# Linear attention: the value mask moved behind a page pair, the sum over sequences moved between two chunk states, the first half of the scores scaled behind the head loop in two parts

## What is computed

```python
k, v = mla_keys_values(cache_ckv_l[phys], cache_kpe_l[phys], kpos, w_ukv, g_kh)
sc = jnp.einsum('bthd,bkhd->bhtk', q, k).astype(jnp.float32) * scale
m_new = jnp.maximum(m, sc.max(axis=-1))
p = jnp.exp(sc - m_new[..., None])
```

```python
inter = jnp.einsum('bthk,bhkv->bthv', qc * jnp.exp(b), s)
s = jnp.exp(bl)[..., None] * s + jnp.einsum('bshk,bshv->bhkv', kc * jnp.exp(bl[:, None] - b), vc)
```

## Time and profile before

| | before |
|---|---|
| median of 3 runs | 1000.68 us (1000.61 to 1001.48) |
| profiled execution, its own time | 1000.3 us |
| its span, first to last instruction | 998.3 us |
| TensorE (PE) busy | 957.6 us, 96% |
| VectorE (DVE) busy | 632.2 us, 63% |
| ScalarE (ACT) busy | 473.9 us, 47% |
| GpSimd (POOL) busy | 129.0 us, 13% |
| TensorE's share of the chain that ended last | 73% |
| VectorE's, GpSimd's share of it | 10%, 5% |

### The profile page before, as it was taken

How to read it: one execution, slowest core, us unless ns; L and a number is a source line. 1 busy time by engine, 2 the same in 40 slices (tenths; PEclk the granted TensorE clock), 3 DMA queues, 4 the chain that set the end, 5 groups by cost and what they waited for, 6 DMA issues and landing times.

```text
span 998.3 us, 17683 instructions
## 1 busy us (share of the span) xinstructions
PE 957.6 (96%) x6795; PEld 880.8 (88%) x6795; DVE 632.2 (63%) x1140; ACT 473.9 (47%) x834; POOL 129.0 (13%) x220
## 2 busy tenths in 40 slices
PE   6999999989998999999999898899999999999997
PEld 6998478787886799999999776799999999999997
DVE  5653897787875479855664743756756766444454
ACT  6433566653442457643434473124755555333353
POOL 3420140000132300000003079100000000000000
PEclk9999999999989999999999999556999999999999
DMA  8570032321258634444444205000343444344431
GB/s 321 202 300 27 17 102 73 112 70 43 96 166 279 232 133 165 167 169 169 169 169 161 93 2 211 11 1 1 138 160 149 170 169 170 137 160 157 158 151 48
DMA packets 34485, 135.42 MB, mean 136 GB/s; under 512 B 5273, under 2 KB 17433, under 8 KB 21858
## 3 DMA queue, kind: packets, MB, share of 16 engines
q1 hardware_dynamic: 28370, 117.37, 32.4%
q0 software_dynamic: 6032, 16.92, 5.1%
HBM read 130.11 MB, written 4.17 MB: 135 GB/s over the span
## 4 chain that ended last, share of the span: by engine, by line
PE 73%; DVE 10%; POOL 5%; issue 5%; ACT 3%; DMA 2%; POOLq 1%; SPq 0%; DVEq 0%; ACTq 0%
PE ps L902 18%; PE ps L904 18%; PE ps L903 18%; POOL arena L805 4%; PE ps L1450 3%; DMA ring<-in_stream 2%; PE ps L1107 1%; PE ps L1458 1%; PE ps L1108 1%; PE ps L1467 1%; PE ps L1109 1%; PE ps L1466 1%; POOLq L726 1%; PE ps L1030 1%; DVE arena L2182 1%
## 5 line engine op out<-in xcount | busy, mean ns | idle before, releaser
L904 PE MATMUL ps<-a2hi_split,ring_split 128*128 128x288 f32 x512 | 150.5, 294 | 0.0
L904 PEld LDWEIGHTS ps<-a2hi_split,ring_split 128*128 128x128 f32 x512 | 96.4, 188 | 0.0
L902 PE MATMUL ps<-nhi_split,hi_split 128*128 128x288 f32 x320 | 95.1, 297 | 0.1
L904 PE MATMUL ps<-nhi_split,ring_split 128*128 128x288 f32 x320 | 94.1, 294 | 0.0
L1992 DVE TENSOR_TENSOR ring_split<-ring,hi_split 128x2048 fp32r<-128x2048 f32 x36 | 82.2, 2286 | 17.8 <-ACT hi_split L1562 17.8
L1562 ACT ACTIVATE hi_split<-ring 128x2048 fp32r<-128x2048 f32 x36 | 68.7, 1910 | 31.9 <-PE ps L904 22.7
L1107 PE MATMUL ps<-sq_split,hT_split 128*128 128x288 f32 (+1 forms) x256 | 78.5, 307 | 5.3 <-DVE pages_lo_split L2164 3.3
L902 PE MATMUL ps<-up_nhi_split,up_hi_split 128*128 128x288 f32 x256 | 76.2, 298 | 0.5 <-DVE arena L2388 0.5
L902 PE MATMUL ps<-a2hi_split,hi_split 128*128 128x288 f32 x256 | 75.8, 296 | 0.0
L1108 PE MATMUL ps<-wuk_lo_split,hT_split 128*128 128x288 f32 (+1 forms) x256 | 75.6, 295 | 0.0
L1562 ACT ACTIVATE up_hi_split<-ring 128x2048 fp32r<-128x2048 f32 x28 | 53.6, 1913 | 46.4 <-PE ps L904 44.7
(11 more groups left out here) (430 smaller groups left out, 2629.8 us busy)
## 6 DMA issues: line engine op xcount, KB each, us to landing
ring<-in_stream SPq DMA_DIRECT2D x96, 1024.0 KB, 4.9
arena<-in_ckvT SPq DMA_DIRECT2D x64, 128.0 KB, 2.1
arena<-in_ckv POOLq DMA_DIRECT2D x26, 128.0 KB, 3.0
ring<-in_ckv POOLq DMA_DIRECT2D x21, 128.0 KB, 2.4
arena<-in_wu POOLq DMA_DIRECT2D x1, 2240.0 KB, 10.0
arena<-in_ckv SPq DMA_DIRECT2D x17, 128.0 KB, 2.9
arena<-in_s POOLq DMA_DIRECT2D x4, 512.0 KB, 4.2
out_gla_s<-arena POOLq DMA_DIRECT2D x4, 512.0 KB, 3.4
```

What stands on the lines that cost most here:

```text
L902: pe.matmul(ps[:, 0:T], wh[:, k, col:col + P], xh, start=first and k == which[0], stop=False)
L904: mm = pe.matmul(ps[:, 0:T], wl[:, k, col:col + P], xh, start=False, stop=last and k == which[-1])
```

## The change

Only VectorE's program changes. Three steps move, none is added or taken away, and no data moves elsewhere:

```diff
-            V.tensor_tensor(vmask, bc(gv[:, 2, 0:GD].unsqueeze(1), [P, NS, GD]), bc(cst("seqmask").unsqueeze(2), [P, NS, GD]), ALU.mult).then_inc(vmask_ready, 1)
             for c in range(2):
...
                                 ALU.mult).then_inc(bank_of(("cross", c)), 1)
-            for c in range(2):
-                copied(dve, ("cross", c))
-            V.tensor_reduce(crossed, own.rearrange("p b v -> p v b"), AX.X, ALU.add).then_inc(crossed_ready, 1)
             for h in range(GH):
 
                 if h == 2:
+                    for c in range(2):
+                        copied(dve, ("cross", c))
+                    V.tensor_reduce(crossed, own.rearrange("p b v -> p v b"), AX.X, ALU.add).then_inc(crossed_ready, 1)
                     key_sums(18, 19)
...
             key_sums(19, 20)
+            V.tensor_tensor(vmask, bc(gv[:, 2, 0:GD].unsqueeze(1), [P, NS, GD]), bc(cst("seqmask").unsqueeze(2), [P, NS, GD]), ALU.mult).then_inc(vmask_ready, 1)
...
-            def scaled_scores(c):
+            def scaled_scores(c, between=(0, 0)):
...
                 link(w)
+                key_sums(*between)
                 m = mx[:, P * c:P * c + P]
...
-                if h == 2:
-                    scaled_scores(0)
...
-            key_sums(24, 29)
+            key_sums(24, 25)
+            scaled_scores(0, (25, 26))
+            key_sums(26, 29)
             maxima(0)
```

## The result

The changed kernel took 974.32 us (971.87 to 975.37) against 1001.08 (1000.61 to 1004.0) beside it, a ratio of 0.9723 with a 95% interval of 0.9697 to 0.975. I had forecast 995.5, and 993.2 as the lower end: the sign was right, the size was not, and nearly all of the gain lies where I had not looked. One fact is needed to read this number, and I only learned it from later comparisons: **both kernels have two outcomes**, one execution after the other on the same chip. Of 101 executions of the kernel before, 58 took 1000.4 to 1007.1 us and 43 took 973.3 to 980.3; of 28 of the changed one, 4 took 999.2 to 1001.1, one 987.4, and 23 took 971.4 to 975.4. The comparison above sets the upper outcome of one against the lower outcome of the other. Between like outcomes the ratio was 0.9964 (0.9942 to 0.9985) in one later comparison and 0.9969 (0.9949 to 0.9989) in another: some 3 us.

What follows compares the result with a forecast made beforehand. It took VectorE's early scores, ahead of GpSimd's page queue and TensorE's pairs, as the bound. Both paths gain about 5.5 us, 4.9 after the weights; summed as 5.0, 1000.3 becomes 995.3, median 995.5, range 993.2 to 998.2.

Steps and rivals of the forecast that it cites:

- the second view: TensorE's timeline to the MLP: scores path ends 2.6 us after the pages; a shift at 326 passes to the end unchanged.
- Chunk states: First chunk copy 2.75 us earlier; TensorE's 1.82 stall becomes 1.7 at pair 19, probably losing the clock; 0.1 us gained.
- rival 1: TensorE keeps the upper clock after the stall moved to pair 19, so 1.75 us stays: 994.0 us; chance 0.20.
- Head 3: State updates without scores ahead: GpSimd's queue gains 2.85 us; TensorE's 2.54 wait before L1238 goes, plus 3.3 from the clock.
- Scores among the pairs: Moved scores delay key sums of pairs 25 and 26: TensorE stalls 0.2 to 0.3 us; pairs end 5.55 earlier.
- Where the paths meet: Before L1270's second half, scores (313.4) and pages (313.45) arrive together, 5.5 us earlier; weights then land 4.9 earlier.
- rival 2: The queue decides: a weight unit runs beside GpSimd's last pages, or weights need 12.4 us; 997.7 us, chance 0.23 with port variant.
- The variant in the port: Moved VectorE work locks GpSimd out of their shared port during page issues, up to 3.5 us: 998.5 us; chance 0.04.
- The sum of 5.0: Whole kernel: 5.0 us off the profiled 1000.3 gives 995.3, median put at 995.5; chance 0.46.
- Rival 3: VectorE can't catch up among pairs 24 to 28: at 3.5 us per pair, 1002.8 us; chance 0.06.

Runs made afterwards that it cites:

- scores_only: The kernel before with only the first scores' scaling moved out of the loop over heads, in two parts behind it: 973.3 to 976.6 us in nine, 987.1 in one.
- b_nudge: The kernel before plus one useless VectorE copy in the first gate's sixth block: four at 974.8 to 977.5 us, two at 1001.7 and 1003.0.
- mask_sum: The kernel before with the value mask and the sum over sequences moved, the scores not: 1003.1 to 1005.1 us in five executions, 974.5 to 975.9 in three.
- a_deal16: The changed kernel with GpSimd issuing 16, not 18, second-half value pages, SyncE the other two: seven of ten at 966.9 to 968.9 us, others 979.9, 981.1, 995.9.
- b_cover: The kernel before with nine filler calls instead of one before the first L1450: nine of ten at 975.4 to 980.0 us, one 1000.0.

## Why the prediction was right and wrong

**The step that failed is a sentence of the second view**: "What comes after 366 starts from TensorE's results, so I let a shift at 326 pass to the end unchanged." It does not pass unchanged. From 571 to 627 TensorE and VectorE run against GpSimd's rotations; 0.1 us of order between two instructions there goes with which wait is the long one, and whether the clock falls in the wait at the stage's door is worth 25 us. The base of the forecast had the same gap: its 1000.68 is the median of three executions that were all of the upper outcome. The page of the kernel before showed the place, in the granted clock of its forty slices:

```profile
PEclk9999999999989999999999999556999999999999
```

Three slices at 5, 5 and 6 tenths, 624 to 699 us, far from the edit, and I did not ask what could end them.

**Chunk states: place right, size wrong.** The stall moved to pair 19's last heads as forecast, but is 1.29 us (at 247.72) and not 1.7, and the clock stayed at 1.00 from 235 to 250. That is rival 1's condition. The new stall is not the only reason for it: the old order, with its wait of 1.81 or 1.82, kept the clock too in two of eight traces (scores_only and b_nudge), the new order in ten of ten. So whether a stall of this length loses the clock was a matter of odds, and the prediction took it as likely.

**Head 3: right.** No wait before L1238, clock 1.00 from 274 to 306, GpSimd's state store at 279.49 (I said 279.3). This execution had begun the chunk states 1.95 us later, so it was better than forecast.

**Scores among the pairs: right.** TensorE waited for no page half from pair 24 on. The first half of L1270 started at 301.09 against 306.01, 6.9 us earlier from the same L1202; 5.55 plus rival 1's 1.75 are 7.3.

**Where the paths meet: wrong.** TensorE was ready at 313.26, but the last page landed at 317.61. I had taken the landing as 3.07 from the earlier trace rows for a page that now had a weight unit beside it. This is the first half of rival 2, at a price of 3.2 us; what I had not priced is the clock's fall in the wait, 0.54 from 318 to 324, 2.6 us more between L1270 and the out-projection (9.95 us, against 7.31 in the earlier trace rows). Together they ate the 5 us: local gain 0.8 to 1.5. The variant in the port did not occur at its price: of 3.5 us at most 0.7 were seen. GpSimd's first two gaps between page issues, beside the moved products, were 1.70 and 2.02 us, against 1.45 and 1.61 before and 1.44 and 1.89 in mask_sum, where the products had not moved; the others were as before (1.13 for most).

**The sum of 5.0** (its own working ends at 4.9) is about what the paths could have given: a_deal16, without that collision and with two pages less in GpSimd's queue, comes out 5.4 to 6.0 earlier. And as a forecast of like against like, 995.5 to 1000.68 is a ratio of 0.9948, inside one of the two later intervals and just outside the other. Some 1.5 to 2.7 of the 3.0 to 3.5 us measured there lie behind the first gate, for a reason that stays open, so that agreement is in part luck.

**Rival 3** did not occur. No rival had the clock of another stage in it.

## What to carry to other kernels

Look in the profile for stretches at the lower clock anywhere in the program, and ask what stands at their door; a wait in front of a long stage of small multiplications can be worth more than the edit one plans, and filler multiplications there cost 0.2% where they weren't needed (b_cover to the kernel before's quicker outcome, 1.0021). If a change brings far more than the path it shortens, run the kernel before again until both its outcomes are seen, and compare like with like. When a queue is made earlier, deal its work anew: the other queue's next transfer starts earlier too.

## What was not expected of the hardware

TensorE stayed at the granted clock 0.50 from 626 to 690 while busy without a gap (40.00 of 40.00 us from 650 on), and was at 1.00 after six filler multiplications. An add of 0.46 us on VectorE took up to 2.55 beside GpSimd's rotations, and a rotation of 2.35 took 2.70; the add had started 0.10 us behind the rotation in the one case and 0.01 ahead of it in the other. An instruction of VectorE that no edit touches started 0.35 us later in all nine traces with the scores' move. A 128 KB page landed in 6.25 us instead of 3.07 beside one 1 MB transfer issued 1.98 us before it.
